# A mixture-of-experts stage: expert rows multiplied by their gates and added into the output in memory, and all experts in one order

## The chip, the cores and the metric

The kernel runs on one core of a Trainium2 chip. The metric is the device time of one execution in microseconds (us). The core has TensorE (PE in the profile; PEld is its weight load), VectorE (DVE), ScalarE (ACT), GpSimd (POOL) and SyncE (SP), and 16 DMA engines that carry out the transfers which SP, ACT and POOL issue. Engines wait for each other by semaphores. PSUM has eight banks of 2 KB per partition; matmul results land there.

## The reference

Two transformer blocks on 512 tokens of width 1024, all in float32. The first block has two kinds of attention and a dense MLP; the second has windowed attention beside an mLSTM, and then a mixture of 32 experts. Only this last part is touched:

```python
def hier_moe(h, w_rg, b_rg, w_re, b_re, w_gate, w_up, w_down):   # h = rmsnorm(x), 512 x 1024
    g_idx = argmax(h @ w_rg + b_rg)                  # one of 4 groups per token
    p_group = softmax(group logits)[g_idx]
    top_v, top_i = top_k(expert logits of that group, 2)          # 2 of its 8 experts
    top_w = softmax(top_v) * p_group                 # the two gates of a token
    # for each expert e, over the rows xs of its tokens:
    ys = (silu(xs @ w_gate[e]) * (xs @ w_up[e])) @ w_down[e]      # 1024 -> 512 -> 1024
    y = zeros.at[row_tok].add(ys * row_w)            # every token gets the sum of its two rows
x = x + y
```

512 tokens with two experts each make 1024 rows over 32 experts, 32 rows each on average. Every expert has three matrices of 2 MB (gate, up, down), read from memory once.

## The kernel before

The stage begins when the router has given every token its two experts. VectorE works out for each (token, choice) its rank among the rows of its expert. An expert has a block of `BLK` = 96 slots, filled from slot 0 by rank; experts with more tokens than 96 would send the rest to overflow blocks at the end (`njobs`), of which there are none with these inputs: each weight matrix is loaded 32 times. A product of two indicator matrices on TensorE (`place_hot`, `block_tok`, L1480) turns this into a table of token numbers, slots by blocks; an empty slot gets a number that is out of bounds, and the indirect transfers leave it out.

Then the experts run one after the other, each engine with its own written-out loop over two buffers `s`:

- POOL: `fetch(b)` copies a column of the table to `idcol` and gathers 96 rows of h by an indirect DMA; `spread(b)` stores the 96 result rows `ys` by an indirect DMA into `y_scratch`, at row (choice x 512 + token). In the loop it does fetch(e+4), spread(e).
- PE: `expert_gate_up(e)` (L1497: slots 0 to 63 against 512 columns of gate and of up, into bank 2; L1502: slots 64 to 95 in four pieces into bank 3), `next_tokens` (L1488: eight transposes of the rows of expert e+1), `expert_down(e-1)` (L1517 into bank 4, L1522 into bank 5), `turn_hidden(e)` (L1511: four transposes of the hidden rows).
- ACT: `hidden_silu` (L1978 after L1497, L1980 after L1502), `rows_a` (L1984, L1985: bank 4 to `ys`).
- DVE: `hidden` (L2825, L2829: silu times up), `turned_tokens` (L2818), `rows_b` (L2840: bank 5 to `ys`), `turned_hidden` (L2835).
- SP: `load_gate_up(e)` waits until gate_up(e-2) is done, since it overwrites those weights, `load_down(e)` until down(e-2) is done. All are in one queue in the order of the code.

The end is special. After turn_hidden(30) PE does down(30) first and then gate_up(31), so that expert 30's rows get to memory early. The rows of expert 31 never go to memory: `last_hot` (96 slots by 512 tokens, with the gates in it, built on DVE at L2855 to L2858 and turned at L1546) spreads them by eight matmuls (L1582) over all eight PSUM banks. SP reads `y_scratch` back (eight transfers, L687), DVE multiplies each by its gate and adds it to `x` (`add_gathered`, L2847), then adds the banks (`add_last`, L2888), and SP stores each of the four tiles of x (L705). `y_scratch` and `over_scratch` are filled with zeros early (L749).

Of the kernel before, what the change touches and what calls it, by code (L numbers as in the profile page):

```python
# [22 lines left out]
F32 = mybir.dt.float32  # L23
I32 = mybir.dt.int32
# [4 lines left out]
P = 128  # L29
D = 1024  # L30
# [22 lines left out]
BLOCKS = NE + MAXJOBS  # L53
# [6 lines left out]
def build(nc, io, out):  # L60
    ctx = ExitStack()
    with ctx:
# [170 lines left out]
        idcol = sb("idcol", [BLK, 6], I32)  # L233
# [6 lines left out]
        def work(*shape):  # L240
# [6 lines left out]
            if len(shape) == 1:  # L247
# [22 lines left out]
        hidT = yTw[:, 1536:1920].rearrange("p (k t) -> p k t", k=4)  # L270
        sga, sgb = yTw[64:128, 1920:2432], yTw[64:128, 2432:2688]
        hid = yTw[0:BLK, 2688:3200]

        hTr = hT[:, :, :].rearrange("p (a c) t -> p a (c t)", a=4)
        yg = [[hTr[:, i, :] for i in range(NT)],
              [stage[:, 0, :], stage[:, 1, :]] + [smb[:, 2 * n:2 * n + 2, :].rearrange("p a b -> p (a b)") for n in range(2)]]
        last_hot = cbuf[:, 3072:3072 + NT * BLK].rearrange("p (i r) -> p i r", i=NT)
        last_hotT = cbuf[0:BLK, 3456:3968]
        LAST_ADDS = [(0, i) for i in range(NT)] + [(1, 0), (1, 1), (1, 2), (2, 0), (1, 3), (2, 1), (2, 2), (2, 3)]
        last_tmp = cbuf[:, 3968:3968 + BLK]  # L280
        r_last = small[:, cur[0]:cur[0] + 2 * NT].rearrange("p (c i) -> p c i", c=2)
        row_ids = small[0:BLK, cur[0] + 2 * NT:cur[0] + 2 * NT + BLOCKS].bitcast(I32)
        id_work = small[0:BLK, cur[0] + 2 * NT + BLOCKS:cur[0] + 2 * NT + 2 * BLOCKS]
        assert cur[0] + 2 * NT + 2 * BLOCKS <= 640

        h_dram = nc.dram_tensor("h_scratch", (SEQ, D), F32, kind="Internal").ap()
        y_dram = nc.dram_tensor("y_scratch", (2 * SEQ, D), F32, kind="Internal").ap()
        over_dram = nc.dram_tensor("over_scratch", (2 * SEQ, D), F32, kind="Internal").ap()
# [26 lines left out]
        def kv_view(c):  # L315
# [49 lines left out]
        last_rows, sel_ready, rank_done, slots_ready, y_zero = (  # L365
            sem("last_rows"), sem("sel_ready"), sem("rank_done"), sem("slots_ready"), sem("y_zero"))
# [7 lines left out]
        y_store = [sem(f"y_store{s}") for s in range(2)]  # L374
        idcol_ready = sem("idcol_ready")

        EXPERT = ("xt", "xT", "gua", "gub", "silua", "silub", "hida", "hidb", "ht", "hT",
                  "downa", "downb", "ysa", "ysb")
        ex = {n: sem(f"ex_{n}") for n in EXPERT}
        ov = {n: sem(f"over_{n}") for n in ("wgu", "wd", "id", "gather", "store", "free")}  # L380
        y_gather = [[sem(f"y_gather{c}_{i}") for i in range(NT)] for c in range(2)]
        add_done, out_store = sem("add_done"), sem("out_store")
# [179 lines left out]
        def _(sp):  # L562
# [84 lines left out]
            source += [io[names[2]].rearrange("l e (k p) n -> (l e) p k n", p=P)]  # L647
# [35 lines left out]
            sp.wait_ge(y_store[1], 16 * (NE // 2 - 1))  # L683
            sp.wait_ge(y_store[0], 16 * (NE // 2))
# [4 lines left out]
            sp.wait_ge(ex["downb"], NE)  # L689
            n = sp.value_load(njobs[0:1, 0:1], min_val=0, max_val=MAXJOBS)  # L690
            with sp.If(n > 0):
                with sp.Fori(0, n) as j:
                    which = sp.value_load(jobs[0:1, bass.ds(j, 1)], min_val=0, max_val=NE - 1)
                    sp.wait_ge(ov["free"], j + 1)
                    for q, nm_ in enumerate(("wgu", "wgu", "wd")):
                        sp.dma_start(views[0][q], source[q][which]).then_inc(ov[nm_], 16)
                sp.wait_ge(add_done, 3 * NT)
                sp.wait_ge(ov["store"], n * 16)
                for c in range(2):
                    for i in range(NT):  # L700
                        sp.dma_start(yg[c][i], over_dram[c * SEQ + i * P:c * SEQ + (i + 1) * P, :]).then_inc(y_gather[c][i], 16)
                sp.wait_ge(add_done, 5 * NT)
            for i in range(NT):
                sp.wait_ge(add_done, LAST_ADDS.index((2, i)) + 1)
                sp.dma_start(out[0, i * P:(i + 1) * P, :], x[:, i, :]).then_inc(out_store, 16)  # L705
# [4 lines left out]
        def _(pool):  # L710
# [37 lines left out]
            for rows_dram in (y_dram, over_dram):  # L748
                pool.dma_start(rows_dram.rearrange("(s j) (q c) -> s (j q) c", s=P, c=256),  # L749
# [2201 lines left out]
```

## Time and profile before

| | us |
|---|---|
| median of 3 runs | 1802.75 (1799.29 to 1803.11) |
| profiled execution, time | 1799.5 |
| its span, first to last instruction | 1797.7 |
| PE busy | 1747.2 (97%) |
| first matmul of expert 0 | at 1222.07 |
| last matmul of expert 31's down product | ends at 1784.7 |

The profile shows one execution: per engine the busy time, the chain of waits that ended last, groups of instructions, waits by releaser, and DMA transfers with their time from issue to landing. "DMA share" is the mean busy share of the 16 DMA engines. A landing time runs until the last of the engines is done with its part of the transfer.

### The profile page before, as it was taken

What the parts mean: (1) busy time and instruction counts of PE and PEld (TensorE: products, weight loads), DVE (VectorE), ACT (ScalarE), POOL (GpSimd) and SP (SyncE); (2) the same over time, 40 slices, a digit from 0 to 9 for tenths busy, and PEclk for the clock granted to TensorE, in tenths of its full rate; (3) what the DMA queues carried; (4) which work ended last, traced back from release to release, by engine and by line L of the source; (5) the groups of instructions that cost most, each with busy time, mean ns of one, the idle gap of its engine ahead of it and who ended that gap; (6) DMA issues with size and microseconds to landing.
All of it is one profiled execution on the core that took longest, in us unless ns stands there. A gap on an engine that the chain in (4) does not pass through costs nothing.

```text
span 1797.7 us, 24219 instructions
## 1 busy us (share of the span) xinstructions
PE 1747.2 (97%) x9718; PEld 1011.3 (56%) x9718; DVE 830.4 (46%) x1691; ACT 386.8 (22%) x835; POOL 161.2 (9%) x183
## 2 busy tenths in 40 slices
PE   7999999999999999999999999978999999999997
PEld 4444455588888888654447884443444444444443
DVE  3486876464445454617754553553222232222224
ACT  4334655200000000223642230021111111111111
POOL 0000000000000000100014130401111111111110
PEclk9999999999999999999999999988999999999999
DMA  5521123201222213261111133544999999999995
GB/s 179 122 64 47 47 73 116 81 25 47 94 94 94 94 66 121 82 259 47 47 47 50 45 109 94 209 166 179 374 384 368 378 365 375 382 372 371 387 384 208
DMA packets 84851, 316.73 MB, mean 176 GB/s; under 512 B 11967, under 2 KB 13116, under 8 KB 76589
## 3 DMA queue, kind: packets, MB, share of 16 engines
q1 hardware_dynamic: 72992, 291.60, 42.9%
q0 software_dynamic: 11056, 22.03, 4.3%
q10 hardware_dynamic: 732, 2.15, 0.3%
q8 instruction: 47, 0.77, 0.2%
q14 instruction: 24, 0.19, 0.0%
HBM read 305.41 MB, written 26.87 MB: 185 GB/s over the span
## 4 chain that ended last, share of the span: by engine, by line
PE 95%; DVE 3%; issue 1%; ACT 1%; DMA 0%; ACTq 0%; SPq 0%; DVEq 0%; POOLq 0%
PE ps L1497 13%; PE ps L1119 11%; PE ps L1075 11%; PE ps L943 8%; PE ps L1502 6%; PE ps L1517 6%; PE ps L1216 6%; PE ps L1363 5%; PE ps L1522 3%; PE ps L979 3%; PE ps L939 3%; PE ps L1402 3%; PE ps L1428 3%; PE ps L1488 1%; PE ps L998 1%; PE ps L1275 1%
## 5 line engine op out<-in xcount | busy, mean ns | idle before, releaser
L1497 PE MATMUL ps<-W,yT 128*64 128x512 f32 x1024 | 229.5, 601 | 1.1 <-ACT yT L1973 0.7
L943 PE MATMUL ps<-hT,W 128*128 128x512 f32 (+1 forms) x336 | 149.3, 596 | 1.5 <-ACT hT L1658 1.5
L1497 PEld LDWEIGHTS ps<-W,yT 128*64 128x64 f32 x1024 | 71.7, 138 | 135.0 <-issue 130.1
L1216 PE MATMUL ps<-hT,W 128*128 128x512 f32 x272 | 122.3, 599 | 1.9 <-DVE yT L2514 1.9
L1517 PE MATMUL ps<-W,yT 128*64 128x512 f32 x512 | 116.9, 598 | 2.5 <-DVE yT L2835 2.5
L1502 PE MATMUL ps<-W,yT 128*32 128x256 f32 x2048 | 117.1, 380 | 0.0
L2840 DVE COPY mix<-ps 32x256 f32<-32x256 f32 x124 | 52.3, 421 | 126.1 <-PE ps L1522 124.8
L2825 DVE TENSOR_TENSOR yT<-yT,ps 64x512 f32<-64x512 f32 x32 | 22.1, 690 | 186.8 <-ACT yT L1978 186.8
L943 PEld LDWEIGHTS ps<-hT,W 128*128 128x128 f32 (+1 forms) x336 | 61.2, 188 | 75.0 <-issue 72.9
L1502 PEld LDWEIGHTS ps<-W,yT 128*32 128x32 f32 x2048 | 63.3, 110 | 64.4 <-issue 26.0
L1216 PEld LDWEIGHTS ps<-hT,W 128*128 128x128 f32 x272 | 50.1, 190 | 65.3 <-issue 62.4
L1075 PE MATMUL ps<-yT,cbuf 128*128 128x256 f32 x384 | 85.5, 379 | 0.0
L1119 PE MATMUL ps<-cbuf,mix 128*128 128x256 f32 x368 | 81.9, 379 | 0.0
L1748 ACT ACTIVATE smb<-ps 128x512 f32<-128x512 f32 x10 | 6.0, 595 | 349.8 <-PE ps L1119 185.3
L1075 PEld LDWEIGHTS ps<-yT,cbuf 128*128 128x128 f32 x384 | 73.0, 190 | 9.9
L1119 PEld LDWEIGHTS ps<-cbuf,mix 128*128 128x128 f32 x368 | 69.9, 190 | 9.5
L1978 ACT ACTIVATE yT<-ps 64x512 f32<-64x512 f32 x32 | 18.8, 589 | 261.5 <-PE ps L1497 261.5
L1517 PEld LDWEIGHTS ps<-W,yT 128*64 128x64 f32 x512 | 33.9, 136 | 61.1 <-issue 54.8
L2829 DVE TENSOR_TENSOR yT<-yT,ps 32x256 f32<-32x256 f32 x64 | 27.0, 422 | 87.1 <-ACT yT L1980 86.7
L1522 PE MATMUL ps<-W,yT 128*32 128x256 f32 x1024 | 61.9, 382 | 0.0
L1674 ACT ACTIVATE yT<-ps 32x512 f32<-32x512 f32 x82 | 48.2, 588 | 44.4 <-PE ps L943 43.6
L979 PE MATMUL ps<-W,hT 128*128 128x512 f32 x128 | 57.7, 600 | 0.0
(456 smaller groups left out, 2659.6 us busy)
## 6 DMA issues: line engine op xcount, KB each, us to landing
W<-in_w_expert_gate SPq DMA_DIRECT2D x32, 2048.0 KB, 10.2
W<-in_w_expert_up SPq DMA_DIRECT2D x32, 2048.0 KB, 15.5
W<-in_w_expert_down SPq DMA_DIRECT2D x32, 2048.0 KB, 15.2
W<-in_w_in SPq DMA_DIRECT2D x16, 2048.0 KB, 7.8
W<-in_w_up SPq DMA_DIRECT2D x8, 2048.0 KB, 7.5
W<-in_w_down SPq DMA_DIRECT2D x8, 2048.0 KB, 7.8
W<-in_w_out SPq DMA_DIRECT2D x4, 2048.0 KB, 8.0
y_scratch<-cmask POOLq DMA_DIRECT2D x1, 4096.0 KB, 18.7
```

Source lines behind the costliest of these rows:

```text
L939: ins = pe.matmul(ps[:, bank, :], hT[:, k, j * P:(j + 1) * P], wv[:, k, :], start=(k == 0), stop=(k == KT - 1))
L943: ins = pe.matmul(ps[0:n, bank, :], wv[:, k, j * P:j * P + n], hT[:, k, :], start=(k == 0), stop=(k == KT - 1))
L979: ins = pe.matmul(ps[:, bank, :], lhs[:, k, i * P:(i + 1) * P], ring_view(c, KT, 512)[:, k, :], start=(k == 0), stop=(k == 7))
L1075: ins = pe.matmul(ps[:, bank, 256 * j:256 * j + 256], lhs[:, k, j * P:(j + 1) * P], rhs[:, k, :], start=(j == 0 and k == 0), stop=(j == 1 ...
L1119: ins = pe.matmul(ps[:, bank, 256 * t:256 * t + 256], lhs[:, k, t * P:(t + 1) * P], rhs[:, k, :], start=(q == 0 and t == 0 and k == 0), st ...
L1216: ins = pe.matmul(ps[:, bank, :], wv[:, k, j * P:(j + 1) * P], hT[:, k, :], start=(k == 0), stop=(k == KT - 1))
L1363: ins = pe.matmul(ps[:, bank, 256 * j:256 * j + 256], lhs[:, k, j * P:(j + 1) * P], rhs[:, k, :], start=(j == 0 and k == 0), stop=(j == 1 ...
L1402: ins = pe.matmul(ps[:, bank, :], ring[c % 2][:, br_ * 2048 + k * 512 + j * P:br_ * 2048 + k * 512 + (j + 1) * P], yT[:, 4 + k, :] if br_ ...
L1497: ins = pe.matmul(ps[64 * part:64 * part + 64, 2, :], xsT[:, s, k, 0:64], wviews[s][part][:, k, :], start=(k == 0), stop=(k == KT - 1))
L1502: ins = pe.matmul(ps[32 * q:32 * q + 32, 3, 0:256], xsT[:, s, k, 64:BLK], wviews[s][q // 2][:, k, 256 * (q % 2):256 * (q % 2) + 256], star ...
L1517: ins = pe.matmul(ps[64 * half:64 * half + 64, 4, :], hidT[:, k, 0:64], wviews[s][2][:, k, half * 512:(half + 1) * 512], start=(k == 0), s ...
L1522: ins = pe.matmul(ps[32 * q:32 * q + 32, 5, 0:256], hidT[:, k, 64:BLK], wviews[s][2][:, k, q * 256:(q + 1) * 256], start=(k == 0), stop=(k ...
```

## The change

- The output tensor `out` takes x itself: SP stores the four tiles of x into `out` as soon as x is final, before the weights of expert 2 are asked for.
- A second small product on TensorE (`place_hot` by `block_weight`, 24 matmuls) gives each slot its gate, kept in `slot_weight`. DVE's `hidden` becomes a `scalar_tensor_tensor` that also multiplies by it, so that result rows come out weighted.
- `spread(b)` is an indirect DMA from `ys` straight into `out` with `compute_op=ALU.add`: each row is added to what the memory holds. Since a token has two rows, `spread(b)` first waits until spread(b-1) has landed (`rows_out`). The scratch tensors, their zero fills, the reads back, and all additions on DVE at the end are gone.
- Every expert is done in one order: gate_up(e), tokens of e+1, down(e-1), turn_hidden(e); the last one too. `last_hot` and its products are gone.
- ACT waits once for both parts of gate_up and does both silus, and it empties both banks of the down product (six copies; DVE does none).
- Two more blocks are fetched at the end (blocks 32 and 33, empty here), for overflow work that starts earlier; the gate_up of expert 30 is cut in two halves for the same reason.
- The down weights are read as `(p k) n` in place of `(k p) n`: 16 KB in one piece per partition where there were four pieces of 4 KB. `hidden` writes its columns in the matching order.

```diff
-            source += [io[names[2]].rearrange("l e (k p) n -> (l e) p k n", p=P)]
+            source += [io[names[2]].rearrange("l e (p k) n -> (l e) p k n", p=P)]
...
+            sp.wait_ge(x_ready, WO_FINAL[-1])
+            for i in range(NT):
+                sp.dma_start(out[0, i * P:(i + 1) * P, :], x[:, i, :]).then_inc(out_store, 16)
...
-            for c in range(2):
-                for i in range(NT):
-                    sp.dma_start(yg[c][i], y_dram[c * SEQ + i * P:c * SEQ + (i + 1) * P, :]).then_inc(y_gather[c][i], 16)
...
-            for i in range(NT):
-                sp.wait_ge(add_done, LAST_ADDS.index((2, i)) + 1)
-                sp.dma_start(out[0, i * P:(i + 1) * P, :], x[:, i, :]).then_inc(out_store, 16)
+            sp.wait_ge(rows_out, 16 * NE)
...
-            def spread(b, s, nth):
-                pool.wait_ge(ex["ysa"], b + 1)
-                pool.wait_ge(ex["ysb"], b + 1)
+            def spread(b, s, nth, landed):
+                pool.wait_ge(ex["ys"], b + 1)
                 pool.tensor_copy(idcol[:, 2 + s:3 + s], row_ids[:, bass.ds(b, 1)]).then_inc(idcol_ready, 1)
                 pool.wait_ge(idcol_ready, nth)
-                spread_rows(s, 2 + s, y_dram, y_store[s])
+                if landed is not None:
+                    pool.wait_ge(rows_out, landed)
+                pool.sem_inc(fetches, 1)
+                pool.indirect_dma_start(out=out[0], out_offset=bass.IndirectOffsetOnAxis(ap=idcol[:, 2 + s:3 + s], axis=0),
+                                        in_=ys[0:BLK, s, :], in_offset=None, bounds_check=SEQ - 1, oob_is_err=False,
+                                        compute_op=ALU.add).then_inc(rows_out, 16)
...
+            pe.wait_ge(slots_ready, 3)
+            for n in range(2 * NT):
+                pe.matmul(ps[64:128, 7, 0:BLOCKS], place_hot[:, n, 0:64], block_weight[:, n, :],
+                          start=(n == 0), stop=(n == 2 * NT - 1))
+            for n in range(2 * NT):
+                for at in (64, 96):
+                    ins = pe.matmul(ps[at:at + 32, 5, 0:BLOCKS], place_hot[:, n, 64:BLK], block_weight[:, n, :],
+                                    start=(n == 0), stop=(n == 2 * NT - 1))
+            ins.then_inc(idT_done, 1)
...
+            def rows(n, s):
+                act.wait_ge(ex["down"], n)
                 act.activation(ys[0:64, s, 0:512], ps[0:64, 4, :], ACT.Copy)
+                act.activation(ys[0:64, s, 512:1024], ps[64:128, 4, :], ACT.Copy)
+                for q in range(4):
+                    ins = act.activation(ys[64:BLK, s, 256 * q:256 * q + 256], ps[32 * q:32 * q + 32, 5, 0:256], ACT.Copy)
+                ins.then_inc(ex["ys"], 1)
...
-                dve.tensor_tensor(hid[0:64, :], sga, ps[64:128, 2, :], ALU.mult).then_inc(ex["hida"], 1)
+                dve.scalar_tensor_tensor(out=hid_k[0:64], in0=by_k(sga), scalar=slot_weight[0][:, bass.ds(e, 1)],
+                                         in1=by_k(ps[64:128, 2, :]), op0=ALU.mult, op1=ALU.mult)
...
-            expert_down(NE - 2, 0, 8 * NE)
-            expert_gate_up(NE - 1, 1, 8 * NE)
-            turn_last_hot([2, 3]).then_inc(turn_done, 1)
-            turn_hidden(NE - 1)
-            expert_down(NE - 1, 1, 8 * NE)
+            expert(NE - 1, 1, 8 * NE, 8 * NE + 16)
+            expert_ahead(NE - 1, 1, 8 * NE)
+            turn_rows(NE - 1)
+            pe.wait_ge(ex["ys"], NE - 1)
+            pe.wait_ge(ex["hT"], NE)
+            pe.wait_ge(wd_load[1], 8 * NE)
+            down(1)
```

On POOL, in the loop over the experts, `fetch` (the COPY of a table column and the gather `mix<-h_scratch`) and `spread` follow each other. Before:

```order
L825 ISA [waits ex_xt]
L825 COPY idcol<-cbuf 96x1
L826 ISA
L819 DMA mix<-h_scratch,idcol 96x1024 [waits idcol_ready]
L836 REGISTER_ALU
L838 ISA [waits ex_ysb,ex_ysa]
L838 COPY idcol<-small 96x1
L839 REGISTER_ALU
L831 DMA y_scratch<-mix,idcol 1024x1024 [waits idcol_ready]
```

The same place in the changed kernel:

```order
L808 ISA [waits ex_xt]
L808 COPY idcol<-small 96x1
L809 ISA
L802 DMA mix<-h_scratch,idcol 96x1024 [waits idcol_ready]
L813 REGISTER_ALU
L814 ISA [waits ex_ys]
L814 COPY idcol<-small 96x1
L815 REGISTER_ALU
L817 REGISTER_ALU [waits idcol_ready]
L819 DMA out_x<-mix,idcol 512x1024 [waits rows_out]
```

The order is the same; the store became the adding transfer into `out_x`, and a wait for the one before it stands ahead of it. What is queued behind it on POOL is the next fetch.

On PE, from the down product of expert 29 to the end of the stage (L1546 turns `last_hot`, L1582 spreads the last rows). Before:

```order
L1517 MATMUL ps<-W,yT 64x512 x8
L1522 MATMUL ps<-W,yT 32x256 x16
L1511 MATMUL ps<-ident,yT 128x96 x4
L1546 MATMUL ps<-ident,cbuf 96x128 x2
L1517 MATMUL ps<-W,yT 64x512 x8
L1522 MATMUL ps<-W,yT 32x256 x16
L1497 MATMUL ps<-W,yT 64x512 x16
L1502 MATMUL ps<-W,yT 32x256 x32
L1546 MATMUL ps<-ident,cbuf 96x128 x2
L1511 MATMUL ps<-ident,yT 128x96 x4
L1517 MATMUL ps<-W,yT 64x512 x8
L1522 MATMUL ps<-W,yT 32x256 x16
```

And now (L1488 and L1492 are gate_up, L1480 turns tokens, L1507 and L1511 are down, L1501 turns the hidden rows):

```order
L1507 MATMUL ps<-W,yT 64x512 x8
L1511 MATMUL ps<-W,yT 32x256 x16
L1501 MATMUL ps<-ident,yT 128x96 x4
L1488 MATMUL ps<-W,yT 64x512 x16
L1492 MATMUL ps<-W,yT 32x256 x32
L1480 MATMUL ps<-ident,mix 128x96 x8
L1507 MATMUL ps<-W,yT 64x512 x8
L1511 MATMUL ps<-W,yT 32x256 x16
L1501 MATMUL ps<-ident,yT 128x96 x4
L1507 MATMUL ps<-W,yT 64x512 x8
L1511 MATMUL ps<-W,yT 32x256 x16
```

The gate_up of expert 31 moved ahead of the down product of expert 30, the transposes of `last_hot` went, and one more set of token transposes came in.

## Rows read from the trace of the kernel before

**Rows 1.** The page, part 2: DMA share in 40 slices of 45 us.
```profile
DMA  5521123201222213261111133544999999999995
```
**Rows 2.** Stretches of the expert stage: span, busy per engine (count), granted clock, DMA share, GB/s.
```profile
1260.00:1500.00 240.00, 240.00 (x2174) 100.59 (x2172) 67.15 (x140) 30.10 (x56) 31.31 (x55) 1.00 0.95 374
1500.00:1740.00 240.00, 240.00 (x2170) 100.26 (x2168) 65.03 (x136) 30.10 (x56) 30.91 (x53) 1.00 0.98 379
```
**Rows 3.** Chain of waits, end of the stage: start, us, what.
```profile
1723.66 7.02 PE ps L1497 x32
...
1741.01 7.02 PE ps L1497 x32
...
1765.90 7.02 PE ps L1497 x32
...
1779.16 3.65 PE ps L1517 x16
1782.81 1.91 PE ps L1522 x32
...
1785.64 7.12 PE ps L1582 x16
```
**Rows 4.** Waits of PE, 1260 to 1800: total us, times, longest.
```profile
PE ps L1517 <- DVE yT L2835: 2.5, 2, 1.8
```
**Rows 5.** DMA issues, 1300 to 1350: count, KB, median us to landing.
```profile
W<-in_w_expert_up SPq DMA_DIRECT2D x3, 2048.0 KB, 14.4
...
y_scratch<-mix,idcol POOLq DMA_INDIRECT x3, 7.0
```
**Rows 6.** DMA issues, 1690 to 1740.
```profile
W<-in_w_expert_up SPq DMA_DIRECT2D x3, 2048.0 KB, 18.6
```
**Rows 7.** DMA issues, 1180 to 1250: the first loads of the loop.
```profile
W<-in_w_expert_gate SPq DMA_DIRECT2D x2, 2048.0 KB, 8.1
W<-in_w_expert_up SPq DMA_DIRECT2D x2, 2048.0 KB, 13.5
```
**Rows 8.** DMA issues, 1757 to 1772: the last down load, nothing else loading.
```profile
W<-in_w_expert_down SPq DMA_DIRECT2D x1, 2048.0 KB, 8.3
```
**Rows 9.** DMA queues, 1300 to 1700: packets, MB, share of 16 engines; then the stores.
```profile
q1 hardware_dynamic: 18693, 144.40, 92.1%
q0 software_dynamic: 5152, 5.30, 4.0%
...
y_scratch<-mix,idcol POOLq DMA_INDIRECT x23, 7.7
```
**Rows 10.** DMA, 1739 to 1757: GB/s in 40 slices of 0.45 us.
```profile
GB/s 455 355 501 455 437 364 473 437 437 400 437 364 400 473 473 237 346 419 364 282 355 419 392 401 428 391 419 255 182 191 164 137 91 73 82 46 27 27 27 9
```
**Rows 11.** Timeline of SP: issue of the last up load, expert 31's.
```profile
1734.72 0.43 SPq L667 DMA_DIRECT2D W<-in_w_expert_up  x1
```
**Rows 12.** Timeline: expert 30's last copies and store, expert 31's last copies.
```profile
1766.04 1.73 DVE L2840 COPY mix<-ps 32x256 f32<-32x256 f32 x4 [5.71 <-PE ps L1522]
...
1767.90 0.18 POOL L838 COPY idcol<-small 96x1 int32<-96x1 int32 x1 [6.05 <-DVE mix L2840]
...
1768.95 0.93 POOL L831 DMA_INDIRECT y_scratch<-mix,idcol  x1 [0.87 <-POOL idcol L838]
...
1784.74 1.55 ACT L2005 ACTIVATE mix<-ps 32x256 f32<-32x256 f32 x4 [0.63 <-PE ps L1522]
```
**Rows 13.** Groups by line, 1260 to 1740: one copy of bank 4 (busy us, mean ns).
```profile
L1985 ACT ACTIVATE mix<-ps 64x512 f32<-64x512 f32 x28 | 16.6, 594 | 0.3
```
**Rows 14.** DMA issues, 1765 to 1798: the last store.
```profile
y_scratch<-mix,idcol POOLq DMA_INDIRECT x1, 3.6
```
**Rows 15.** Timeline, start of the stage.
```profile
1211.61 2.79 PE L1480 MATMUL ps<-cbuf 128*96 128x42 f32 x16 [5.16 <-DVE cbuf L2793]
...
1219.86 1.51 PE L1488 MATMUL ps<-ident,mix 96*128 96x96 f32 x8 [5.46 <-DMA mix<-h_scratch,idcol]
...
1222.07 9.79 PE L1497 MATMUL ps<-W,yT 128*64 128x512 f32 x32 [0.70 <-ACT yT L1973]
```

More of the change, by code:

```diff
@@ L842, in _ @@
             for s in range(2):
-                gather_tokens(s, s, gather[s])
+                gather_tokens(s)
             pool.wait_ge(ids_ready, 2)
-            fetch(2, 0, 1)
-            fetch(3, 1, 2)
-            with pool.Fori(0, NE // 2 - 2) as it:
-                for s in range(2):
-                    fetch(it * 2 + (4 + s), s, it * 4 + (3 + 2 * s))
-                    spread(it * 2 + s, s, it * 4 + (4 + 2 * s))
-            for e in range(NE - 4, NE - 1):
-                spread(e, e % 2, NE - 1 + e)
+            fetch(2, 0, 1, 1)
@@ new lines, in _ @@
+            fetch(3, 1, 2, 2)
+            fetch(4, 0, 3, 3)
+            pool.wait_ge(out_store, 16 * NT)
+            spread(0, 0, 4, None)
+            fetch(5, 1, 5, 4)
+            spread(1, 1, 6, 16)
+            with pool.Fori(1, NE // 2 - 2) as it:
+                for s in range(2):
+                    fetch(it * 2 + (4 + s), s, it * 4 + (3 + 2 * s), it * 2 + (3 + s))
+                    spread(it * 2 + s, s, it * 4 + (4 + 2 * s), it * 32 + 16 * s)
+            fetch(NE, 0, 2 * NE - 5, NE - 1)
@@ L853, in _ @@
+            for e in range(NE - 4, NE - 2):
+                spread(e, e % 2, NE + e, 16 * e)
+            fetch(NE + 1, 0, 2 * NE - 2, NE + 1)
+            for e in range(NE - 2, NE):
+                spread(e, e % 2, NE + e + 1, 16 * e)
             pool.wait_ge(job_ready, 1)
@@ L1549, in _, with expert_ahead @@
-            next_tokens(0, 16)
-            pe.wait_ge(route_act, 7)
-            expert_gate_up(0, 0, 16)
-            next_tokens(1, 16)
-            turn_hidden(0)
-            expert_gate_up(1, 1, 16)
-            next_tokens(0, 32)
-            expert_down(0, 0, 16, first=True)
-            turn_hidden(1)
+                pe.wait_ge(gather[1 - s], loads_ahead)
+                turn_tokens(1 - s)
+            def expert_ahead(e, s, loads_ahead, second=False):
+                pe.wait_ge(ex["hT"], e)
+                pe.wait_ge(wd_load[1 - s], loads_ahead)
+                if not second:
+                    pe.wait_ge(ex["ys"], e - 1)
+                down(1 - s)
@@ L1558, in _, with turn_rows @@
+            def turn_rows(e):
+                pe.wait_ge(ex["hid"], e + 1)
+                turn_hidden()
+            pe.wait_ge(gather[0], 16)
+            turn_tokens(0)
+            pe.wait_ge(route_act, 7)
+            expert(0, 0, 16, 16)
+            turn_rows(0)
+            expert(1, 1, 16, 32)
+            expert_ahead(1, 1, 16, second=True)
+            turn_rows(1)
             with pe.Fori(1, NE // 2 - 1) as it:
                 for s in range(2):
-                    expert_gate_up(it * 2 + s, s, it * 16 + 16)
@@ L1572, in _ @@
[L1572 to L1584 removed]
+                    expert(it * 2 + s, s, it * 16 + 16, it * 16 + (16 + 16 * s))
@@ new lines, in _ @@
+                    expert_ahead(it * 2 + s, s, it * 16 + 16 * s)
+                    turn_rows(it * 2 + s)
+            pe.wait_ge(ex["xT"], NE - 1)
+            pe.wait_ge(wg_load[0], 8 * NE)
+            pe.wait_ge(wu_load[0], 8 * NE)
+            gate_up(0, range(4)).then_inc(ov["half_free"], 1)
+            gate_up(0, range(4, KT))
+            pe.wait_ge(gather[1], 8 * NE)
+            turn_tokens(1)
+            expert_ahead(NE - 2, 0, 8 * NE - 16)
+            turn_rows(NE - 2)
+            expert(NE - 1, 1, 8 * NE, 8 * NE + 16)
@@ L1989, in _ @@
                 if e:
[L1990 removed]
+                    rows(e, 1 - e % 2)
             with act.Fori(1, NE // 2 - 1) as it:
@@ L2868, in _ @@
+            for e in range(2):
+                expert(e, e)
             with dve.Fori(1, NE // 2 - 1) as it:
                 for s in range(2):
[L2870 to L2879 removed]
```

324 lines of the change are left out of this document (104 added, 220 removed).

## The prediction

> **What bounds the kernel now.** I read the slices first: from about 1250 us to the end, the expert stage, the DMA engines stand at 9 tenths and more, as nowhere else [rows 1]. The stretches say that in this stage PE is busy for 240 of 240 us, and the DMA engines for 95 and then 98% [rows 2]. So two things run side by side at nearly the same speed. The waits say which one leads: PE waits for nothing inside the loop; what it waits for lies at the end of the stage [rows 4]. One expert takes 1741.01 - 1723.66 = 17.35 us of PE [rows 3].
>
> Then I asked how much cover the transfers have. The up weights of expert e are asked for when gate_up(e-2) is done and are needed when gate_up(e) starts. For the last one: issued at 1734.72 [rows 11]; with gate_up(31) one period after gate_up(30), it is needed at 1741.01 + 17.35 = 1758.4. That gives 23.6 us. Landing takes 13.5 us at the start of the stage [rows 7], 14.4 a little later [rows 5] and 18.6 at its end [rows 6]. The reader is to see the trend: the slowest DMA engine falls behind by 5.1 us over 30 experts, 0.17 us each, and nobody notices, because the cover was 10.1 us (23.6 - 13.5) and 5.0 is left.
>
> Which engine that is can be guessed from the last loads: their rate falls from about 420 GB/s in steps to 27, a sixteenth of 432 [rows 10]. So at the end one DMA engine works alone while fifteen are done. What makes engines unequal is the row transfers: a block's slots are filled from slot 0, and on average 32 of 96 hold a row. If 96 slots are dealt to 16 engines in order (my assumption), each gets six, the first five engines have all theirs filled and the last ten have none. Then the first engine carries six gathered and six stored rows for every expert, whatever its count. (The Trainium skill, "DMA: Bandwidth & Descriptors", section "Why a DMA increments its semaphore by 16 and not by 1", says that the largest number up to 16 that divides the partitions is taken, which is 16 for 96; the drain in rows 10 fits it, but does not show it.)
>
> **The change part by part.** All against the profiled execution, 1799.5 us (span 1797.7).
>
> *The adding transfer.* A row is 4 KB. An engine at 27 GB/s [rows 10] moves 4096 B in 0.152 us; by the share of the row queue, 4.0% of 16 x 400 us = 256 us for 5.30 MB, it is 0.198 us [rows 9]. Low end: the addition is done on the way, and a row costs what a store costs, 0 more. Middle: the row must be fetched from memory before it can be added to, so one row read comes on top, as in a gather: 6 x 0.152 = 0.91 us per expert on the first engine. High end: read, read and write each count, two rows more, 1.82 us. I take the middle, since the extra work is one read of the same size as the gather's. (The Trainium skill, "Collectives: The Full Stack", section on the bandwidth ceiling, says that an adding transfer runs at half the rate of a copy since both sources go through the same ring. That would be the middle value too; nothing in this trace adds in memory, so nothing here shows it.)
>
> *Down weights in pieces of 16 KB.* A lone down load, in 4 KB pieces, lands in 8.3 us [rows 8]; a gate load in 16 KB pieces, in 8.1 [rows 7]. I take -0.25 us per expert, between 0 and -0.4.
>
> *What both do to the stage.* The busiest engine gets 0.17 + 0.91 - 0.25 = 0.83 us per expert behind PE. Over 30 experts that is 24.9 us; 10.1 are covered; PE must wait for the other **14.8 us**, in the second half or so of the stage, ahead of gate_up. With the low end nothing is left over (0). With the high end 30 x 1.74 - 10.1 = 42 us. Break-even with what the end gives back (below) is an addition of about 0.5 us per expert, 0.08 us per row.
>
> *Waits inside the loop.* The silu of the first 64 slots now waits for all of gate_up. The hidden rows are then ready about 0.6 (silu) + 0.7 + 0.9 (products) = 2.2 us after it, and the token copies another 1 us later; PE has tokens and a down product to do until 0.9 + 5.6 = 6.5 us after it (3.65 + 1.91 for down [rows 3]). Covered: 0. The same holds for ACT's six copies, 2 x 0.59 + 1.55 = 2.7 us [rows 12, 13] in 17.35. The gates cost no instruction; the product on DVE only changes its form. The strided write of the hidden rows I take at 0; even doubled (+1.6 us) it stays under 6.5.
>
> *The wait of one spread for the one before.* Behind it on POOL stands the next fetch, and PE waits for that. A store lands in 7.7 us in the middle of the stage [rows 9]; the next is issued 17.35 us later. If a row takes twice as long it lands in about 9 to 11. Covered.
>
> *The start.* Between the table product and the arrival of the first rows PE idles from 1214.4 to 1219.86 [rows 15]. Into this gap go 48 short matmul instructions (24, two passes each). At 2.79/16 = 0.17 us each they take 8.4 us and delay PE by 2.9; with the 32 narrow ones at a third of it, 4.6, and no delay. DVE then does its two gate copies and the overflow list (2 us) before the first token copy: up to 2 us more. Expert 0 has no down product to hide its hidden rows: +0.9. Against that, PE runs expert 0 slowly: 9.79 us [rows 15] for what takes 7.02 later [rows 3]. A PE that does not idle may get its clock back earlier: down to -3.3. Together from -2.5 to +4.5; I take +1. The store of x and the two gone zero fills lie in stretches where DMA is at 1 to 5 tenths [rows 1]: 0.
>
> *The end.* Before, after turn_hidden(30): down(30), gate_up(31), down(31) until 1784.72, copies, spreading product until 1792.76, last addition, store, 1797.7. Now, with weights in time: gate_up(31) at 1758.4, tokens until 1769.8, down(30) until 1775.4, ACT's copies until 1778.2 (the banks must be empty), down(31) until 1783.8, copies until 1786.6. POOL needs 1.2 us to issue (1767.77 to 1768.95 [rows 12]): 1787.8. A last store lands in 3.6 us [rows 14], an adding one in 3.6 to 6: end at 1791.4 to 1793.8. That is -6.3 to -3.9, of which I take **-4.5**. The previous spread, issued at 1779.4, has 8 us to land.
>
> *Sum:* 1799.5 + 1 + 14.8 - 4.5 = 1810.8. The median of the runs lies 3.25 above the profiled time, so I forecast **1814 us**, 0.6% slower.
>
> **The rivals.**
>
> *The cover holds.* The addition costs under 0.06 us per row, or the rows are spread evenly over the engines, so that 32 x 0.152 / 16 = 0.3 us per expert is all that comes on top and the piece size takes it back. For it: PE waits for no weights now, and 5 us are left. Against it: the trend in landing and the lone engine. Then 1799.5 + 1 - 4.5 = 1796.0, as a median 1799: this is 0.2% faster, and that is also about what a measurement of this kernel can tell from no change. With the clock back early, 1796. This is the case on the other side; it decides when the added time per expert stays under 10.1/30 - 0.17 + 0.25 = 0.42 us.
>
> *The chain of additions sets the pace.* Each spread waits for the one before, and it takes 2.1 us from there to the next. If an adding transfer takes over 15.2 us to land, the period is that landing plus 2.1. With 18 us: 20.1 - 17.35 = 2.75, x 29 = 80 us, about 1880. For it: a row's read from memory may not be pipelined with the next. Against: the gathers read rows without it, and 7.7 us would have to double.
>
> *The end gives nothing.* If the last adding transfer takes 10 us on idle queues, the end comes at 1798 and the -4.5 becomes 0. This shifts the other cases by 4 us, no more.
>
> **How the numbers follow.** Forecast (first engines overloaded, middle to high price): 0.45, from 1804 to 1842. Cover holds: 0.43, 1796 to 1803, of which 0.27 beyond 0.2% faster and 0.16 within. Chain: 0.12, over 1850. Range 1796 to 1845: it leaves out the chain and a little below. The forecast case has a small part within 0.2%, 0.02. So faster 0.27, same 0.18, slower 0.55.
>
> **What the profile of the changed kernel would show.** Right: waits of PE ahead of gate_up for `in_w_expert_up` or `in_w_expert_gate`, none in the first third of the stage, about 0.8 us each later; landing of up loads rising to 23 us and staying there; DMA share 0.99; period 18.2. Wrong in size: another period. Wrong in kind: no wait of PE for weights, up loads landing under 23 us (cover holds); or POOL's spread waiting for `out_x`, and fetches late (chain). The end: last down product to the end of the span 8 to 10 us, where it was 13.

## The result, and the profile after

| | before | after |
|---|---|---|
| median of 6 runs, us | 1802.7 (1799.29 to 1803.84) | 1810.11 (1808.75 to 1811.67) |
| ratio, 95% interval | | 1.0043 (1.003 to 1.0055) |
| profiled execution, time and span | 1799.5, 1797.7 | 1808.93, 1806.9 |

The changed kernel is 0.4% slower: 7.4 us by the medians, 9.2 by the spans of the two profiled executions. Four stretches of PE's work split these 9.2 us. The marks are the first matmuls of expert 0, of expert 1 and of expert 30, and the end of the span.

| stretch | before | after | difference |
|---|---|---|---|
| until expert 0 | 1222.07 | 1219.67 | -2.40 |
| expert 0 | 15.82 | 17.55 | +1.73 |
| experts 1 to 29 | 503.05 | 512.40 | +9.35 |
| expert 30 to the end | 56.76 | 57.28 | +0.52 |

The waits of PE from 1225 us on come first (total us, times, longest); before, no wait for weights stood there [rows 4].

```profile
PE ps L1488 <- DMA W<-in_w_expert_up: 7.4, 7, 2.6
PE ps L1507 <- ACT mix L1963: 2.4, 1, 2.4
PE ps L1501 <- DVE yT L2813: 2.4, 1, 2.4
PE ps L1488 <- DVE yT L2797: 0.5, 1, 0.5
```

The timeline of PE shows the first and the last of the seven waits for up weights. The start of expert 21 is the first place; up to there PE ran without a gap.

```profile
1584.65 7.09 PE L1488 MATMUL ps<-W,yT 128*64 128x512 f32 x32 [0.43 <-DMA W<-in_w_expert_up]
...
1713.50 8.52 PE L1488 MATMUL ps<-W,yT 128*64 128x512 f32 x32 [2.59 <-DMA W<-in_w_expert_up]
```

The last one costs more than its 2.59 us: behind it the product takes 8.52 us where 7.09 are usual. The stretches around it (busy time per engine, then the granted clock, DMA share, GB/s) show a granted clock of 0.50 behind the wait, the lower level (1.2 GHz), and then its return.

```profile
1710.00:1713.00 3.00, 0.91 (x13) 0.36 (x4) 0.56 (x1) 2.44 (x6) 0.00 (x0) 1.00 1.06 350
1713.00:1716.00 3.00, 2.50 (x6) 0.85 (x8) 0.00 (x0) 0.24 (x1) 1.59 (x2) 0.50 1.00 320
1716.00:1718.00 2.00, 2.00 (x12) 0.75 (x10) 0.00 (x0) 0.00 (x0) 0.05 (x1) 0.89 0.95 401
```

So 7.4 us of waits, 1.4 of clock and 0.5 unaccounted for are the 9.3 us. Where the waits come from is seen in the landing of the up loads, here at 1300, 1500 and 1690 us (one line of each answer; count, KB, median us). They started at 13.3, much as before (13.5 [rows 7]); the kernel before had 14.4 at 1300 and 18.6 at 1690 us [rows 5, 6].

```profile
W<-in_w_expert_up SPq DMA_DIRECT2D x3, 2048.0 KB, 16.9
```
```profile
W<-in_w_expert_up SPq DMA_DIRECT2D x3, 2048.0 KB, 22.4
```
```profile
W<-in_w_expert_up SPq DMA_DIRECT2D x2, 2048.0 KB, 24.7
```

The queues from 1300 to 1700 us are the counterpart of [rows 9]. The row queue q0 moved a little less (5.17 MB for 5.30) and took 5.4% of the engines' time for 4.0%.

```profile
q1 hardware_dynamic: 9775, 142.38, 88.7%
q0 software_dynamic: 5092, 5.17, 5.4%
```

5.4% of 16 x 400 us is 346 us for 1262 rows of 4 KB, 0.274 us each; before it was 0.198. Half of the rows are gathers. If these cost what they did, a stored row costs 2 x 0.076 = 0.15 us more.

The stretches of the stage: DMA share 0.94 in both, PE busy for 232.6 of the second 240 us [rows 2].

```profile
1260.00:1500.00 240.00, 240.00 (x2172) 100.47 (x2170) 56.34 (x84) 49.50 (x112) 37.75 (x55) 1.00 0.94 373
1500.00:1740.00 240.00, 232.57 (x2066) 99.16 (x2066) 52.34 (x78) 45.95 (x104) 38.15 (x54) 0.99 0.94 364
```

### The profile page after: what moved, and what is told of

Read it like the earlier page. It is cut to its first block, busy times and chain, and to the rows that moved or that the text cites. A ratio compares the mean times of both kernels' runs of the same rounds, so it can differ in the third digit from the quotient of the medians.

```text
span 1806.9 us, 24219 instructions
## 1 busy us (share of the span) xinstructions
PE 1747.3 (97%) x9754; PEld 1016.0 (56%) x9754; DVE 788.2 (44%) x1550; ACT 428.6 (24%) x958; POOL 177.5 (10%) x187
## 4 chain that ended last, share of the span: by engine, by line
PE 90%; DMA 6%; DVE 2%; issue 1%; ACT 1%; SPq 0%; POOL 0%; POOLq 0%; ACTq 0%; DVEq 0%
PE ps L1488 11%; PE ps L1058 11%; PE ps L1102 11%; PE ps L926 8%; PE ps L1199 6%; DMA W<-in_w_expert_up 6%; PE ps L1492 6%; PE ps L1346 5%; PE ps L1507 5%; PE ps L962 3%; PE ps L922 3%; PE ps L1385 3%; PE ps L1411 3%; PE ps L1511 2%; PE ps L1210 2%; PE ps L981 1%
## 5 line engine op out<-in xcount | busy, mean ns | idle before, releaser
L1488 PE MATMUL ps<-W,yT 128*64 128x512 f32 x1024 | 231.0, 604 | 8.6 <-DMA W<-in_w_expert_up 7.4
L2808 DVE SCALAR_TENSOR_TENSOR yT<-yT,ps 64x512 f32<-64x512 f32 x32 | 35.7, 1115 | 359.1 <-ACT yT L1955 359.1
L1488 PEld LDWEIGHTS ps<-W,yT 128*64 128x64 f32 x1024 | 74.7, 139 | 140.7 <-issue 136.4
L1507 PE MATMUL ps<-W,yT 128*64 128x512 f32 x512 | 118.6, 606 | 2.4 <-ACT mix L1963 2.4
L1492 PE MATMUL ps<-W,yT 128*32 128x256 f32 x2048 | 117.4, 381 | 0.0
L1492 PEld LDWEIGHTS ps<-W,yT 128*32 128x32 f32 x2048 | 63.2, 110 | 65.0 <-issue 26.8
L1507 PEld LDWEIGHTS ps<-W,yT 128*64 128x64 f32 x512 | 34.3, 138 | 62.2 <-issue 56.1
L1511 PE MATMUL ps<-W,yT 128*32 128x256 f32 x1024 | 61.9, 382 | 0.0
L1960 ACT ACTIVATE mix<-ps 64x512 f32<-64x512 f32 x32 | 18.9, 590 | 175.8 <-PE ps L1511 175.8
L962 PE MATMUL ps<-W,hT 128*128 128x512 f32 x128 | 57.7, 600 | 0.0
L922 PE MATMUL ps<-W,hT 128*128 128x512 f32 x128 | 56.9, 596 | 0.0
```

The lines of the kernel that those rows point to most:

```text
L922: ins = pe.matmul(ps[:, bank, :], hT[:, k, j * P:(j + 1) * P], wv[:, k, :], start=(k == 0), stop=(k == KT - 1))
L962: ins = pe.matmul(ps[:, bank, :], lhs[:, k, i * P:(i + 1) * P], ring_view(c, KT, 512)[:, k, :], start=(k == 0), stop=(k == 7))
L1488: pe.matmul(ps[64 * part:64 * part + 64, 2, :], xsT[:, s, k, 0:64], wviews[s][part][:, k, :], start=(k == 0), stop=(k == KT - 1))
L1492: ins = pe.matmul(ps[32 * q:32 * q + 32, 3, 0:256], xsT[:, s, k, 64:BLK], wviews[s][q // 2][:, k, 256 * (q % 2):256 * (q % 2) + 256], star ...
L1507: pe.matmul(ps[64 * half:64 * half + 64, 4, :], hidT[:, k, 0:64], wviews[s][2][:, k, half * 512:(half + 1) * 512], start=(k == 0), stop=(k ...
L1511: ins = pe.matmul(ps[32 * q:32 * q + 32, 5, 0:256], hidT[:, k, 64:BLK], wviews[s][2][:, k, q * 256:(q + 1) * 256], start=(k == 0), stop=(k ...
```

## The experiments

Each kernel was timed in rounds beside the kernel before on the same chip, with 4 runs (b_add), 11 (a_plain, a_dealt, b_dealt) or 5 (the others). Medians and ratios to the kernel before (95% interval) of all of them:

| label | what | median us | ratio |
|---|---|---|---|
| a_plain | changed kernel, plain stores | 1798.41 | 0.9982 (0.9973 to 0.9991) |
| a_dealt | changed kernel, dealt slots | 1798.75 | 0.9979 (0.997 to 0.9988) |
| b_dealt | kernel before, dealt slots | 1800.97 | 0.9993 (0.9984 to 1.0002) |
| b_add | kernel before, adding stores | 1821.08 | 1.0104 (1.0089 to 1.012) |
| a_best | a_dealt, another end | 1794.8 | 0.9965 (0.9952 to 0.9979) |
| a_best2 | a_best, 4 KB pieces | 1793.74 | 0.9958 (0.9944 to 0.9972) |
| a_kp_hid | changed kernel, 4 KB pieces | 1814.15 | 1.0071 (1.0057 to 1.0085) |
| a_zero | changed kernel, zero fills back | 1814.56 | 1.0066 (1.0053 to 1.008) |
| a_nojobs | changed kernel, no overflow code | 1810.56 | 1.0048 (1.0033 to 1.0062) |
| a_best3 | a_best2, no overflow code | 1793.7 | 0.9951 (0.9937 to 0.9965) |

**Is it the addition?** a_plain takes it out:

```diff
                                         in_=ys[0:BLK, s, :], in_offset=None, bounds_check=SEQ - 1, oob_is_err=False,
-                                        compute_op=ALU.add).then_inc(rows_out, 16)
+                                        ).then_inc(rows_out, 16)
```

> The changed kernel with the row transfers storing instead of adding (what is left out: the additions, so the output holds one expert's rows in place of the sum). Theory (uneven engines: each adding row costs the first DMA engine about 0.15 us more, six per expert): PE's waits for in_w_expert_up, 9.3 us in the loop, vanish, the up loads at 1690 us land in 18 to 19 us as before the change, where they took 24.7, and the end is 1 to 2 us shorter; together 1798 to 1801 us against 1810 of the changed kernel, which is faster than the kernel before (1803). Rival (the additions cost nothing, and the down weights in 16 KB pieces or the extra gathers make the loads late): the waits and 1808 to 1810 us stay.

Measured 1798.41 us, 11.7 less than the changed kernel. No wait for weights is left; its two longest, one for ACT's copies and one for DVE's hidden product of expert 0, are in the changed kernel as well:

```profile
PE ps L1507 <- ACT mix L1963: 2.4, 1, 2.4
PE ps L1501 <- DVE yT L2813: 2.4, 1, 2.4
```

The up loads at 1690 us land in 16.0 us, and q0 takes 4.0% again:

```profile
W<-in_w_expert_up SPq DMA_DIRECT2D x3, 2048.0 KB, 16.0
```

With plain stores the rest of the change gains 4.3 us.

The other way round, b_add puts the addition into the kernel before:

```diff
-                                        bounds_check=2 * SEQ - 1, oob_is_err=False).then_inc(landed, 16)
+                                        bounds_check=2 * SEQ - 1, oob_is_err=False, compute_op=ALU.add).then_inc(landed, 16)
```

> The kernel before with the additions alone: its row transfers add into the zeroed scratch rows in place of storing. Theory (uneven engines): the first engine falls behind by 0.17 + 0.9 = 1.1 us per expert; 10 of 32 us are covered, so 1803 + 15 to 22 = 1818 to 1825 us, with waits of PE ahead of gate_up for weights from about 1400 us on; more than in the changed kernel, since the down weights still come in 4 KB pieces. Rival (pieces cost nothing): 1811 to 1814 us. Rival (it is the rest of the change that makes the loads late): 1803 us.

Measured 1821.08 us, 18.4 more than the kernel before. Two of its waits:

```profile
PE ps L1497 <- DMA W<-in_w_expert_up: 12.6, 12, 2.6
PE ps L1517 <- DMA W<-in_w_expert_down: 4.2, 1, 4.2
```

The sum came out in the expected range; the waits began at 1518 us, expert 17, and not at 1400. The two runs together show that it is the addition that makes the loads late enough for PE to wait.

**Is it one engine, or all of them?** Dealing puts the row of rank r into slot 6 x (r mod 16) + r / 16, so that with six slots per DMA engine in order every engine gets its share. Every row still goes where it went.

```diff
-                dve.tensor_tensor(place_hot[:, four, :], bc(r_slot[:, four], BLK),
-                                  iot[:, 0:BLK].unsqueeze(1).broadcast_to([P, NT, BLK]), ALU.is_equal).then_inc(slots_ready, 1)
+                for i in range(four.start, four.stop):
+                    ins = dve.tensor_scalar(place_hot[:, i, :].rearrange("p (a b) -> p a b", b=6),
+                                            iot[:, 0:BLK].rearrange("p (b a) -> p a b", b=6), r_slot[:, i:i + 1], None, ALU.is_equal)
+                ins.then_inc(slots_ready, 1)
```

> The changed kernel with additions, but an expert's rows dealt over its 96 slots (rank r in slot 6 x (r mod 16) + r / 16), so that filled slots are spread over the 16 DMA engines if these take six slots each in order. Theory (uneven engines): the added 32 x 0.15 us per expert are shared by 16 engines, 0.3 us each; no wait of PE for weights in the loop, up loads at 1690 us land in under 17 us, about 1800 us. Rival (all engines together are at their limit, 94% busy): the waits of 9 us stay, 1808 to 1811 us. Second rival (slots go to engines in turn, and the first slots were spread already): dealing would put the filled slots on fewer engines and the time would rise above 1815 us.

Measured 1798.75 us. The additions are all there and cost what they cost (queue line of a_dealt, 1300 to 1700), yet the up loads at 1690 us land in 13.4 us and no wait for weights is left:

```profile
q0 software_dynamic: 5172, 5.30, 5.6%
```
```profile
W<-in_w_expert_up SPq DMA_DIRECT2D x3, 2048.0 KB, 13.4
```

All engines together were not at their limit: with the bytes of the kernel before and 1.6 points more time in q0, PE is busy for 240 of 240 us in both halves of the stage, at 0.95 and 0.98 DMA share.

> The kernel before with the same dealing of rows over the slots. Theory (uneven engines): the time stays, since its transfers were hidden (1801 to 1804 us), but the landing of the up loads at 1690 us falls from 18.6 to at most 14.5 us, where it was at the start of the stage, and the drain of the last loads no longer ends with one engine alone. Rival (all engines alike fall behind): the landing stays at 18 to 19 us.

b_dealt has the same edit in `place_hot` and in `last_hot`. Measured 1800.97 us, the same time within the interval. The lines are of 1300 and 1690 us: the loads no longer fall behind, where the kernel before went from 14.4 to 18.6 [rows 5, 6].

```profile
W<-in_w_expert_up SPq DMA_DIRECT2D x3, 2048.0 KB, 12.7
```
```profile
W<-in_w_expert_up SPq DMA_DIRECT2D x3, 2048.0 KB, 13.6
```

The drain is steeper too. Its rates from 1739 to 1757 us fall from 273 to 36 in four slices, where [rows 10] shows 13 slices from 255 to 9:

```profile
GB/s 546 437 364 364 510 437 437 364 510 437 364 437 437 473 328 437 437 346 319 209 346 346 355 410 428 374 428 437 428 428 273 173 100 36 0 0 36 0 0 0
```

That engines are loaded unevenly, and that the order of the slots decides it, is shown by these two pairs; which slot goes to which engine is not seen in the profile directly.

**Pieces of the down weights.** a_kp_hid reads them in four 4 KB pieces again and writes the hidden rows contiguously, in the changed kernel:

```diff
-            source += [io[names[2]].rearrange("l e (p k) n -> (l e) p k n", p=P)]
+            source += [io[names[2]].rearrange("l e (k p) n -> (l e) p k n", p=P)]
...
-                hid_k = hid.rearrange("r (k p) -> r p k", k=4)
+                hid_k = hid.rearrange("r (p k) -> r p k", k=4)
```

> The changed kernel with the down weights in 4 KB pieces and the hidden rows written contiguously, slots not dealt. Theory (16 KB pieces save 0.25 us per expert on the engine that is behind): the waits of PE for in_w_expert_up rise from 9 to 14 to 18 us and begin at about expert 17 instead of 21; less 1 us at the start: 1814 to 1818 us. Rival (pieces cost nothing): 1808 to 1810 us.

Measured 1814.15 us, 4.0 more. The waits grew to this line, from 1516.67 us on (expert 17):

```profile
PE ps L1488 <- DMA W<-in_w_expert_up: 12.8, 12, 2.2
```

At 1500 us the up loads landed in 25.2 us for 22.4. Over the 16 experts until then that is 2.8 / 16 = 0.17 us per expert for the pieces. This is an average and a rough one: at 1300 us the difference was 1.9 already, at 1400 it was 2.2, and at 1500 PE's waits set in, which hold the lag down. The same edit on dealt slots is a_best2, below; there it costs nothing that could be seen.

**The zero fills.** a_zero puts the two fills of 4 MB back, with POOL's wait for them:

```diff
+            for rows_dram in (y_dram, over_dram):
+                pool.dma_start(rows_dram.rearrange("(s j) (q c) -> s (j q) c", s=P, c=256),
+                               cmask[:, 0:256].unsqueeze(1).broadcast_to([P, 32, 256])).then_inc(y_zero, 16)
             then(pool.memset(yT[0:MROWS, 0:6, :], 0.0))
```

> The changed kernel with the two zero fills of 4 MB at about 755 us put back. Theory (they took transfer time from the weights of the block before, and PE lost 2.4 us there): the stage begins 2 to 3 us later, 1812 to 1813 us. Rival (the gain before the stage is from elsewhere, the fills cost nothing): 1809.5 to 1810.5 us.

Measured 1814.56 us, 4.4 more where 2 to 3 were expected. The two profiled executions lie 8.0 us apart, and that of a_zero was the slowest of its five runs: 5.0 ahead of the stage (expert 0 at 1224.70) and 2.7 in the stage (10.1 us of waits for up loads for 7.4). Of the first part 4.2 us stand at the place of the fills: half is a later start of PE's transposes, half is the product behind them (15.70 us for 13.90). There the granted clock was 0.79 from 760 to 768 us; the kernel before has 1.00 in that stretch and 14.00 us for the product, with the same fills. A fill at 755 us does not explain the second part; it and the rest of the first I take for scatter between executions, which is not shown. What the fill does was not what I had written. Three timelines show it: DVE and POOL before,

```profile
750.26 0.75 DVE L2066 TENSOR_SCALAR stage<-x,small 128x1024 f32<-128x1024 f32 x1
...
755.40 6.07 DVE L2066 TENSOR_SCALAR stage<-x,small 128x1024 f32<-128x1024 f32 x1
```
```profile
753.96 0.93 POOL L746 DMA_DIRECT2D W<-bias_scratch  x1 [394.47 <-DVE x L2088]
754.89 1.69 POOL L749 DMA_DIRECT2D y_scratch<-cmask  x1
756.47 1.79 POOL L749 DMA_DIRECT2D over_scratch<-cmask  x1
758.03 2.89 POOL L751 MEMSET yT<- 36x3072 f32 x1
```

DVE after,

```profile
755.32 2.71 DVE L2035 TENSOR_SCALAR stage<-x,small 128x1024 f32<-128x1024 f32 x1
```

and DVE, then PE, of a_zero:

```profile
749.53 0.75 DVE L2042 TENSOR_SCALAR stage<-x,small 128x1024 f32<-128x1024 f32 x1
...
754.68 6.06 DVE L2042 TENSOR_SCALAR stage<-x,small 128x1024 f32<-128x1024 f32 x1
```
```profile
760.80 1.09 PE L885 MATMUL ps<-ident,stage 128*128 128x128 f32 x8 [1.91 <-DVE stage L2042]
```

One VectorE instruction that takes 0.75 us alone takes 6.07 while POOL issues its transfers and clears a buffer, and ends 0.5 us after POOL's clearing does. Without the fills POOL is through 3.4 us sooner, DVE too, and PE's wait of 1.91 us ahead of its transposes is gone, which stood in the kernel before as it does here. The transfers themselves play no part: in the kernel before the two fills landed only 18.7 and 28.9 us after their issue, long after DVE and PE had gone on. It is POOL's instructions that hold VectorE. (The Trainium skill, "SBUF — State Buffer", section "Who interferes with whom", says that a VectorE `tensor_scalar` in a two-port mode and GpSimd share a pair of ports that one of them takes for a whole instruction, while the other is fully blocked. The 6.07 us beside the 0.75 agree with it.)

**The end.** a_best has the dealt slots, and for experts 30 and 31 ACT empties bank 4 as soon as it is filled, DVE copies half of bank 5, and POOL fetches the last column of the table ahead of its wait for the rows. Its core:

```diff
-                rows(e + 1, e % 2)
+                act.wait_ge(rows_a_ready, e - (NE - 3))
+                act.activation(ys[0:64, s, 0:512], ps[0:64, 4, :], ACT.Copy)
+                act.activation(ys[0:64, s, 512:1024], ps[64:128, 4, :], ACT.Copy)
+                act.wait_ge(ex["down"], e + 1)
+                for q in range(2):
+                    ins = act.activation(ys[64:BLK, s, 256 * q:256 * q + 256], ps[32 * q:32 * q + 32, 5, 0:256], ACT.Copy)
...
+            def rows_b(e):
+                dve.wait_ge(ex["down"], e + 1)
+                for q in range(2, 4):
+                    ins = dve.tensor_copy(ys[64:BLK, e % 2, 256 * q:256 * q + 256], ps[32 * q:32 * q + 32, 5, 0:256])
```

> The changed kernel with dealt slots and another end: for experts 30 and 31 ACT takes the first bank of the down product as soon as it is ready, and VectorE copies half of the second bank; POOL fetches the last column of token numbers before it waits for the rows. Theory of the end (its 4.5 us were lost to a 2.4 us wait of PE for ACT's copies, to the granted clock that fell behind it, 5.35 in place of 3.65 us for one product, and to 2.7 us of copies plus 1.1 us on POOL after the last product): the wait falls to under 1 us, the product takes 3.65 us again, and the last adding transfer is issued 2.5 to 3 us after the last product instead of 4.0; 4.5 to 6 us less than the dealt kernel's 1798.8, so 1793 to 1794.5 us. Rival (the end is set by how long the last additions take to land, 7 to 9 us, and they are not sooner done since they wait for the ones before): 1797 to 1799 us.

Measured 1794.8 us, 0.3 over the expected range and 4.0 less than a_dealt by the medians (2.5 by the ratios to the kernel before). The last down product in the changed kernel, and in a_best:

```profile
1787.11 5.35 PE L1507 MATMUL ps<-W,yT 128*64 128x512 f32 x16 [2.44 <-ACT mix L1963]
1792.39 1.93 PE L1511 MATMUL ps<-W,yT 128*32 128x256 f32 x32
```
```profile
1777.64 3.65 PE L1519 MATMUL ps<-W,yT 128*64 128x512 f32 x16 [1.37 <-DVE yT L2845]
1781.22 1.93 PE L1525 MATMUL ps<-W,yT 128*32 128x256 f32 x32
```

The wait is 1.4 us for 2.4 (I had expected under 1), the product takes 3.65 us again, and POOL issues the last transfer at 1785.03 us, 1.9 us after the last product ends (1781.22 + 1.93), less than the 2.5 to 3 expected. In the changed kernel it was 4.0 us (1798.33 after 1794.32):

```profile
1798.33 1.44 POOL L819 DMA_INDIRECT out_x<-mix,idcol  x1 [0.90 <-POOL idcol L814]
```

That the shorter wait is what kept the clock up is not shown: a_nojobs, below, and a_kp_hid have the wait of 2.44 us and 3.65 us behind it too. The line of a_nojobs:

```profile
1790.80 3.65 PE L1485 MATMUL ps<-W,yT 128*64 128x512 f32 x16 [2.44 <-ACT mix L1925]
```

> As the last kernel, and the down weights again in 4 KB pieces with the hidden rows written contiguously. Theory (the strided write costs VectorE 1115 in place of some 700 ns, 650 in place of 430, and only experts 0 and 31 show it; with dealt slots the pieces are hidden): expert 0 is 0.8 to 1.2 us shorter, nothing else moves: 1792 to 1794 us, 1 us below the last kernel. Rival (the multiplication by the gate is what makes the VectorE instruction long): 0 us, within 0.3 of the last kernel. Second rival (4 KB pieces cost every engine): landing of the up loads rises through the stage by over 3 us.

Measured 1793.74 us, 1.1 less than a_best by the medians, which the intervals do not tell from nothing. At the place of it, PE's wait for the hidden rows of expert 0, it is 0.7 us: 1.8 where a_best has 2.4. The up loads at 1690 us land in 13.9 us, so the pieces cost nothing. The wait, and the hidden product of expert 0 on DVE, changed kernel and a_best2:

```profile
PE ps L1513 <- DVE yT L2838: 1.8, 1, 1.8
```
```profile
1233.70 1.09 DVE L2808 SCALAR_TENSOR_TENSOR yT<-yT,ps 64x512 f32<-64x512 f32 x1 [14.13 <-ACT yT L1955]
```
```profile
1234.33 0.75 DVE L2833 SCALAR_TENSOR_TENSOR yT<-yT,ps 64x512 f32<-64x512 f32 x1 [14.32 <-ACT yT L1971]
```

The stride costs 0.34 us here and the multiplication by the gate 0.06 (before: 0.69, a plain product). Both have an effect on PE only where no down product stands between, at expert 0. This is the fastest kernel of the study together with a_best3: 8 to 9 us under the kernel before, and additions in memory.

**The last 3 us.** In the changed kernel SP, after the last rows have landed, waits another 3.0 us for PE's sequencer; in the kernel before that wait is 0.2. The two answers (SP, from 1770 us):

```profile
SPq L62 <- DMA out_x<-mix,idcol: 35.4, 1, 35.4
SPq L62 <- PEq L62: 3.0, 1, 3.0
```
```profile
SPq L62 <- DMA out_x<-x: 2.9, 1, 2.9
SPq L62 <- PEq L62: 0.2, 1, 0.2
```

My theory was the jump over the code for overflow blocks. a_nojobs and a_best3 leave that code out:

```diff
-            pe.wait_ge(job_ready, 1)
-            n = pe.value_load(njobs[0:1, 0:1], min_val=0, max_val=MAXJOBS)
-            with pe.If(n > 0):
...
-                    down(0)
```

> The changed kernel without the code for overflow blocks behind the last expert on every engine (left out: rows beyond 96 per expert, of which these inputs have none). Theory (the end is 3 us longer than reckoned because, after the last additions have landed, SP still waits 3.0 us for PE's sequencer, which in the kernel before was 0.2, and that time is the jump over the overflow code): the wait goes to under 0.5 us and the time falls by about 3 us, from 1810 to 1807. Rival (that wait belongs to how every program with this end closes): 3 us stay, 1809 to 1811 us.

> The fastest kernel so far (dealt slots, new end, 4 KB pieces with contiguous hidden rows) with the same code left out. Theory: 1793.7 - 3.4 = 1790 to 1791 us. Rival: 1793 to 1794.5 us.

Measured 1810.56 and 1793.7 us: nothing gained, and the waits are still 3.0 and 3.3 us. The theory fell. The wait is there in each kernel whose last transfer is issued by POOL, adding or not (2.9 to 3.7 us, 3.7 in a_plain), and not in the kernel before, b_dealt and b_add, whose last transfers SP issues (0.2). These two groups differ in the rest of the change as well, so POOL's issue is not shown to be the reason. What PE's sequencer does in it stays open.

## Why the prediction was right or wrong

The side, the mechanism and the place were right; of the sum of +11.3 us on the profiled time the measured +9.4 is made up differently.

- *The engines are unequal, and the first ones carry the rows* (assumed): shown, by a_dealt and b_dealt.
- *An adding row costs one more row read, 0.152 us*: measured 0.15.
- *Pieces, -0.25 us per expert*: 0.17 by a_kp_hid, roughly. Right in sign, and of the right size.
- *Stage, +14.8*: measured +9.3. The term is too large in the part before the cover is used up. The reckoning had 0.83 us per expert from the start, which would use up 10.1 us in 12 experts; it took 21. In b_add 1.1 us per expert would have done it in 9; it took 17. Once PE waits, the size fits: 9.3 us over the ten starts from expert 21 to 30 are 0.9 each. The landing rose by 22.4 - 13.3 = 9.1 us in 16 experts, 0.57 each. The mis-sized term is the 0.91 us per expert for the addition. a_plain differs by it alone, and the changed kernel's up loads land later than its by 3.9 us at 1300, 6.3 at 1400 and 6.8 at 1500 us (22.4 for 15.6): near the reckoned rate in the first experts, but 6.8 / 16 = 0.43 each in all. b_add against the kernel before gives 4.6, 7.3 and 9.4 us. Nor is the lag of the kernel before an even 0.17 each: its landings at 1225, 1300, 1400, 1500, 1600 and 1690 us are 13.5, 14.4, 13.7, 15.6, 16.1 and 18.6. Why the lag builds up more slowly than it costs later was not settled; no run here varied how many rows an expert has. The DMA share, forecast as 0.99, was 0.94. The price of the clock (1.4 us behind the longest wait) was not in the sum.
- *Start, +1*: +1.7 in expert 0. The 48 short matmul instructions took 1.94 + 1.39 = 3.3 us, less than the 4.6 to 8.4 reckoned, and lay in the gap as said. Expert 0 has no cover for its hidden rows. The expected +0.9 did not have the strided write, put at 0: DVE's chain there takes 0.4 and 0.5 us longer in its two parts (1.09 for 0.69, 1.32 for 0.86). The two together are the +1.7.
- *Zero fills, 0*: this step failed. It asked only whether the DMA engines had time. The fills held POOL's instruction stream, POOL held a VectorE instruction, and PE waited 1.91 us for that; the changed kernel comes 2.4 us earlier to the stage.
- *End, -4.5*: this step failed: +0.5. Against the terms, from the first matmul of expert 30: the last down product ended after 44.7 us where 42.8 was reckoned, mostly because the product behind the wait ran for 5.35 us instead of 3.65; copies and POOL's issue took what was reckoned (4.0); the last rows landed 5.6 us after the issue (1806.9 - 3.0 - 1798.33), within the 3.6 to 6 and 0.2 over what -4.5 stands for; and then came the 3.0 us of SP's last wait, which the sum did not have. 1.9 + 0.2 + 3.0 make up the difference of 5.0 to -4.5, to a tenth.
- *The wait of a spread for the one before*: never late. POOL's waits in the stage are for ACT's copies, PE's transposes and its own column copies, none for the additions before. The chain of additions does not set the pace.
- *The cover holds* (0.43): it did not, but its condition "or the rows are spread evenly over the engines" is a_dealt, and the 1799 us given for it are the 1798.75 measured. That its end gains 4.5 us was wrong there too; the fills and the spread of the profiled executions around their medians made up for it: the kernel before lies 3.2 us above its own profiled execution in the median and a_dealt 1.4 below.

The smaller stage, the earlier start and the missing gain of the end offset each other in part: that 1814 comes so near to 1810.11 is in part luck, since the terms are further off.

## What to carry to other kernels

Where an indirect transfer leaves most of its slots empty, the filled ones should be spread over the DMA engines: with 32 of 96 slots filled from the front, an extra 0.15 us per row cost 11 us here, and none at all with the same rows dealt out. "The DMA is idle there" is not enough to cost a transfer at nothing when GpSimd issues it: look also at what the issuing engine holds up. At the end of a kernel, count what comes behind the last landing, and take the copies between two dependent products off one engine, since their wait can cost the clock too.

## What the runs showed of the hardware

- An indirect transfer of 4 KB rows that adds costs 0.27 us per row averaged with the gathers, 0.15 more per stored row than one that stores (if the gathers cost the same), and POOL's issue of it takes 1.44 us for 0.93 (a_plain).
- A wait of PE of 1.9 to 2.6 us can be followed by a lower granted clock (0.50 and 0.53 in the stretches behind two waits of the changed kernel, 0.79 behind one of a_zero) and 1.4 to 1.8 us of loss. It need not be: a_kp_hid and a_nojobs had the same 2.44 us wait at the end and 3.65 us for the product behind it.
- One VectorE `tensor_scalar` of 0.75 us took 6.07 beside GpSimd's transfer issues and memset, and 2.71 beside one transfer issue and the memset; in both it ended 0.55 us after the memset.
- A VectorE product of 64 x 512 whose neighbouring results go to columns 128 apart takes 1.09 us for 0.75.
